# One core, hybrid decoder block: six levels of gated recurrence scores become two products of 192 queries, a step of the compression is moved, two slabs change places

## The reference, cut to what matters

```python
f = lb + (1.0 - lb) * jax.nn.sigmoid(f_logits)
logf, k = jnp.log(f), 1.0 - f
...
A = jnp.cumsum(lf, axis=2)
rel = jnp.where(tri[:, :, None], A[:, :, :, None, :] - A[:, :, None, :, :], -jnp.inf)
att = jnp.einsum('bhtd,bhsd,bhtsd->bhts', qq, kk, jnp.exp(rel))
o_intra = jnp.einsum('bhts,bhse->bhte', att, vv)
```

```python
ck = jnp.einsum('bcpgd,pde->bcge', kc[:, cidx] + pe_k[:, None, :], w_ck)
cv = jnp.einsum('bcpgd,pde->bcge', vc[:, cidx] + pe_v[:, None, :], w_cv)
```

## Time and profile before

| | us |
|---|---|
| median of 3 runs | 487.16 |
| lowest and highest | 487.15, 487.28 |
| the profiled execution, its own time | 487.02 |
| its span in the trace | 485.2 |
| PE busy | 476.9 (98%) |
| DVE busy | 341.4 (70%) |
| ACT busy | 264.3 (54%) |
| POOL busy | 158.1 (33%) |

### The profile page before, as it was taken

One profiled execution on the slowest core, in us unless ns is written; L12 is line 12 of the kernel. 1 busy time (PEld: TensorE's weight loads), 2 busy tenths in 40 slices (PEclk: granted clock), 3 DMA queues, 4 the chain that ended last, 5 costly groups with the idle time before them and its releaser, 6 DMA issues.

```text
span 485.2 us, 9672 instructions
## 1 busy us (share of the span) xinstructions
PE 476.9 (98%) x3974; PEld 465.2 (96%) x3974; DVE 341.4 (70%) x577; ACT 264.3 (54%) x397; POOL 158.1 (33%) x157
## 2 busy tenths in 40 slices
PE   9999999999999999999999999999999999999995
PEld 8999999999999999889999999999999999999995
DVE  4998967678976475797796747878584257655653
ACT  6887755286572737544565445576554245433531
POOL 1073810806200009990156424436745120000000
PEclk9999999999999999999999999999999999999999
DMA  9956552453453665455455344243525535677502
GB/s 294 337 173 192 178 173 63 132 169 109 154 174 95 198 145 174 122 172 179 147 161 187 92 125 134 88 140 122 169 94 174 173 117 188 218 228 249 174 1 86
DMA packets 77030, 76.43 MB, mean 158 GB/s; under 512 B 6783, under 2 KB 75775, under 8 KB 76987
## 3 DMA queue, kind: packets, MB, share of 16 engines
q1 hardware_dynamic: 76699, 75.64, 50.1%
q10 hardware_dynamic: 288, 0.18, 0.2%
HBM read 74.77 MB, written 1.05 MB: 156 GB/s over the span
## 4 chain that ended last, share of the span: by engine, by line
PE 94%; DVE 2%; ACT 2%; issue 1%; DVEq 0%; ACTq 0%
PE ps L986 75%; PE ps L1011 4%; PE ps L1154 3%; PE ps L1105 2%; PE ps L1094 1%; PE ps L1179 1%; PE ps L1173 1%; PE ps L1121 1%; DVE WL L621 1%; PE ps L1012 1%; PE ps L1108 1%; PE ps L1027 1%; PE ps L1122 1%; PE ps L1123 1%; PE ps L1054 1%
## 5 line engine op out<-in xcount | busy, mean ns | idle before, releaser
L986 PE MATMUL ps<-hH,WL 128*128 128x256 f32 x696 | 198.3, 289 | 0.9 <-DVE WL L621 0.9
L986 PE MATMUL ps<-hL,WH 128*128 128x256 f32 x696 | 197.0, 284 | 0.0
L986 PE MATMUL ps<-hH,WH 128*128 128x256 f32 x696 | 197.0, 284 | 0.0
L621 DVE TENSOR_TENSOR WL<-W,WH 128x2048 fp32r<-128x2048 f32 x66 | 152.9, 2316 | 19.6 <-PE ps L986 17.4
L427 ACT ACTIVATE WH<-W 128x2048 fp32r<-128x2048 f32 x66 | 124.6, 1888 | 44.8 <-PE ps L986 43.2
L986 PEld LDWEIGHTS ps<-hL,WH 128*128 128x128 f32 x696 | 132.8, 191 | 1.1 <-issue 1.0
L986 PEld LDWEIGHTS ps<-hH,WL 128*128 128x128 f32 x696 | 131.6, 191 | 2.3 <-DVE WL L621 1.1
L986 PEld LDWEIGHTS ps<-hH,WH 128*128 128x128 f32 x696 | 132.8, 191 | 0.0
L388 POOL TENSOR_SCALAR R<-R,st 128x256 f32<-128x256 f32 x32 | 29.2, 922 | 82.0 <-DVE st L797 82.0
L986 PE MATMUL ps<-bH,WL 128*128 128x256 f32 x192 | 54.9, 286 | 0.0
L986 PE MATMUL ps<-bH,WH 128*128 128x256 f32 x192 | 54.3, 283 | 0.0
(11 more groups left out here) (192 smaller groups left out, 776.9 us busy)
## 6 DMA issues: line engine op xcount, KB each, us to landing
W<-w_in SPq DMA_DIRECT2D x49, 1024.0 KB, 5.2
W<-w_branch SPq DMA_DIRECT2D x12, 1024.0 KB, 5.1
W<-w_out SPq DMA_DIRECT2D x4, 1024.0 KB, 5.8
R<-x SPq DMA_DIRECT2D x2, 512.0 KB, 4.6
W<-w_in SPq DMA_DIRECT2D x2, 512.0 KB, 6.7
R<-cmp_w SPq DMA_DIRECT2D x2, 512.0 KB, 8.3
OC<-pool_w SPq DMA_DIRECT2D x4, 256.0 KB, 5.9
...
```

The lines of the kernel that those rows point to most:

```text
L621: dve.tensor_tensor(WL[:, s % 2, :, 0:n], W[:, s % 3, :, 0:n], WH[:, s % 3, :, 0:n], ALU.subtract).then_inc(s_lo, 1)
L986: mm = pe.matmul(o, l, r, start=(at == 0 if mixed else k == 0 and j == 0), stop=(at == len(order) - 1 if mixed else k == KC - 1 and j == 2))
```

## The change

**Scores.** The levels 32, 16, 8, 4 become two steps of radix 4, with blocks of b = 16 and b = 4 tokens. In a group of four blocks, keys of block j reach queries of blocks j+1 to 3: six block pairs, so `REACH` holds 6b columns for 4b tokens, 192 for 128. `OWN` holds the keys. PE does two products of 192 queries, one of 64 (level 64, now in `HALF`) and one of 128 (blocks of 4, now into the next accumulator bank). Level 128 lies in `TOP`, in the tile `CVD`. POOL writes 4096 elements for a pair of heads in 12 instructions where it wrote 3584 in 12, and ACT's exponential takes 4096 where it took 3584.

**Compression.** ACT copies kc and vc out of the accumulator (`RAW`), and DVE builds the inputs from the copy in `late` of slabs 20 to 23 (`windows`), 4 additions in each.

**Order.** ks and kw become slabs 24 and 25, q3 slab 26. In slab 25 DVE does `lo(27)` ahead of `read(25)`. The copy of the compressed values (CV) moves from slab 28 to 27.

```diff
-LEVELS = (128, 64, 32, 16, 8, 4)
-NLV = len(LEVELS)
-SMALL_K, SMALL_Q = NLV, NLV + 1
+RADIX = (16, 4)
+STEPS = ((0, 3, 1), (3, 2, 2), (5, 1, 3))
...
-    out += [("q", n, "in", C_Q + n * SLAB) for n in (0, 1, 3)]
-    out += [("ks", 0, "in", C_KS), ("kw", 0, "in", C_KW)]
+    out += [("q", n, "in", C_Q + n * SLAB) for n in (0, 1)]
+    out += [("ks", 0, "in", C_KS), ("kw", 0, "in", C_KW), ("q", 3, "in", C_Q + 3 * SLAB)]
...
-CK, CV, CX, SC, TURN = 27, 28, 29, 31, 34
+CK, CV, CX, SC, TURN = 27, 27, 29, 31, 34
+WIN = 20
...
-                for i, b in enumerate(LEVELS):
...
+                b, n = 64, 2 * T // 128
...
+                for r, b in enumerate(RADIX):
+                    n = 2 * T // b
+                    av = a2.rearrange("p (n w) -> p n w", w=b)
+                    pool.tensor_tensor(OWN[p % 2][r].rearrange("p h (n w) -> p (h n) w", w=b),
+                                       k2.rearrange("p (n w) -> p n w", w=b),
+                                       av[:, :, b - 1:b].to_broadcast((P, n, b)), ALU.add)
+                    aw = a2.rearrange("p (n j w) -> p n j w", j=4, w=b)
+                    to = REACH[p % 2][r].rearrange("p h (n j w) -> p (h n) j w", j=6, w=b)
+                    for at, count, far in STEPS:
+                        pool.tensor_tensor(to[:, :, at:at + count], aw[:, :, far:4],
+                                           aw[:, :, 0:count, b - 1:b].to_broadcast((P, n // 4, count, b)), ALU.subtract)
...
-                        q = QK[p % 2]
-                        act.activation(q[:, 0, :, P:T], HA[:, 2 * p:2 * p + 2, P:T], ACT.Exp)
+                        act.activation(TOP[p % 2][:, :, P:T], HA[:, 2 * p:2 * p + 2, P:T], ACT.Exp)
                         for e in range(2):
...
+                        act.activation(DEC[p % 2], DEC[p % 2], ACT.Exp).then_inc(s_hexp, 1)
...
+                elif kind in ("kc", "vc"):
+                    act.activation(RAW[kind == "vc"], bank(s), ACT.Copy).then_inc(s_read_a, 1)
...
-                        for i, b in enumerate(LEVELS):
-                            ev = QK[h // 2 % 2][:, i, h % 2].rearrange("p (n w) -> p n w", w=2 * b)
+                        e, hp = h // 2 % 2, h % 2
+                        for b, to in ((128, TOP), (64, HALF)):
+                            ev = to[e][:, hp].rearrange("p (n w) -> p n w", w=2 * b)
                             qv = HQ[:, h].rearrange("p (n w) -> p n w", w=2 * b)
                             dve.tensor_tensor(ev[:, :, b:2 * b], ev[:, :, b:2 * b], qv[:, :, b:2 * b], ALU.mult)
-                        sq_ = QK[h // 2 % 2][:, SMALL_Q, h % 2]
+                        for r, b in enumerate(RADIX):
+                            qv = HQ[:, h].rearrange("p (n j w) -> p n j w", j=4, w=b)
+                            ev = REACH[e][r][:, hp].rearrange("p (n j w) -> p n j w", j=6, w=b)
+                            for at, count, far in STEPS:
+                                dve.tensor_tensor(ev[:, :, at:at + count], ev[:, :, at:at + count], qv[:, :, far:4],
+                                                  ALU.mult)
+                        sq_ = SMALL_Q[e][:, hp]
                         dve.tensor_tensor(sq_, sq_, HQ[:, h], ALU.mult).then_inc(s_hmul, 1)
...
                     link(dve.copy_predicated(PM[:, u % 2, 0:P], K[:, K_BLOCK:K_BLOCK + P].bitcast(mybir.dt.uint32),
-                                             ps[:, b0, K_BLOCK:K_BLOCK + P]))
-                    for lv in range(1, NLV):
-                        b = LEVELS[lv]
-                        r = slice(0, b if lv == 1 else P)
-                        to = PM[r, u % 2, 0:P].rearrange("p (n w) -> p n w", w=2 * b)[:, :, b:2 * b]
-                        c = slice(64 * (lv - 1), 64 * lv)
-                        last = dve.copy_predicated(to, K[r, c].bitcast(mybir.dt.uint32).rearrange(
-                            "p (n w) -> p n w", w=b), ps[r, b0, c].rearrange("p (n w) -> p n w", w=b))
-                        if lv < NLV - 1:
-                            link(last)
-                    last.then_inc(s_hmask, 1)
+                                             ps[:, b0 + 1, P:2 * P]))
+                    for r, b in enumerate(RADIX):
+                        c = slice(192 * r, 192 * r + 192)
+                        to = PM[:, u % 2, 0:P].rearrange("p (n j w) -> p n j w", j=4, w=b)
+                        on = K[:, c].bitcast(mybir.dt.uint32).rearrange("p (n j w) -> p n j w", j=6, w=b)
+                        src = ps[:, b0, c].rearrange("p (n j w) -> p n j w", j=6, w=b)
+                        for at, count, far in STEPS:
+                            link(dve.copy_predicated(to[:, :, far:4], on[:, :, at:at + count], src[:, :, at:at + count]))
+                    dve.tensor_copy(PM[0:64, u % 2, 64:P], ps[0:64, b0, 384:448]).then_inc(s_hmask, 1)
...
+            def windows(v, r):
+
+                dve.wait_ge(s_read_a, ACT_READS[WHERE[("vc" if v else "kc", 0)]])
+                pos = V[:, V_PEK + CB * v:V_PEK + CB * v + CB].rearrange("p (r j k) -> p r k j", r=2, k=2)
+                raw = RAW[v].rearrange("p (c t) -> p c t", c=2)
+                win = raw[:, :, CS * r:CS * r + CS * NCMP].rearrange("p q (c j k) -> p k j q c", j=CS // 2, k=2)
+                to = cpe[:, v, 8 * r:8 * r + 8].rearrange("p j (q e) c -> p e j q c", e=2)
+                for e in range(2):
+                    h = slice(64 * e, 64 * e + 64)
+                    for k in range(2):
+                        pv = pos[h, r, k].rearrange("p (j q c) -> p j q c", q=1, c=1)
+                        last = dve.tensor_tensor(to[64 * k:64 * k + 64, e], win[h, k],
+                                                 pv.to_broadcast((64, CS // 2, 2, NCMP)), ALU.add)
+                last.then_inc(s_win, 1)
+
             def late(s):
+                if WIN <= s < WIN + 4:
+                    windows((s - WIN) // 2, (s - WIN) % 2)
...
@@ -910,10 +933,12 @@
                 if mixing(s - 1):
                     lo(s + 1)
                 mix(s)
+                if s == WHERE[("kw", 0)]:
+                    lo(s + 2)
                 read(s)
                 if s == LAST:
                     merged_lo(3)
-                if s + 2 < NS and not mixing(s):
+                if s + 2 < NS and not mixing(s) and s != WHERE[("kw", 0)]:
                     lo(s + 2)
                 late(s)
...
-                q = QK[p % 2]
-                for lv in range(1, NLV):
-                    b = LEVELS[lv]
-                    t = q[:, lv, hp, P * i:P * i + P]
-                    up = t.rearrange("p (n w) -> p n w", w=2 * b)[:, :, b:2 * b]
-                    pe.matmul(ps[:, b0, 64 * (lv - 1):64 * lv], t, up, start=(lv == 1), stop=False)
-                mm = pe.matmul(ps[:, b0, K_BLOCK:K_BLOCK + P], q[:, SMALL_K, hp, P * i:P * i + P],
-                               q[:, SMALL_Q, hp, P * i:P * i + P], start=False, stop=True)
+                e, t = p % 2, slice(P * i, P * i + P)
+                for r in range(2):
+                    pe.matmul(ps[:, b0, 192 * r:192 * r + 192], OWN[e][r][:, hp, t],
+                              REACH[e][r][:, hp, 192 * i:192 * i + 192], start=(r == 0), stop=False)
+                pe.matmul(ps[:, b0, 384:448], HALF[e][:, hp, t], HALF[e][:, hp, P * i + 64:P * i + P],
+                          start=False, stop=True)
+                mm = pe.matmul(ps[:, b0 + 1, P:2 * P], SMALL_K[e][:, hp, t], SMALL_Q[e][:, hp, t],
+                               start=True, stop=(i == 0))
                 if i:
-                    mm = pe.matmul(ps[:, b0 + 1, 0:P], q[:, 0, hp, 0:P], q[:, 0, hp, P:T], start=True, stop=True)
+                    mm = pe.matmul(ps[:, b0 + 1, 0:P], TOP[e][:, hp, 0:P], TOP[e][:, hp, P:T], start=False, stop=True)
                 mm.then_inc(s_hp, 1)
...
-                pe.wait_ge(s_read_v, DVE_READS[WHERE[("vc", 0)]])
+                pe.wait_ge(s_win, 4)
```

More of the change, by code:

```diff
@@ L35 @@
 GATES = 3 * HEADS
-K_MASK, K_ID, K_ONE = 0, 448, 576
-K_BLOCK = K_MASK + 64 * (NLV - 1)
-K_CMASK, K_VALID, K_COUNT = 704, 734, 736
-K_ROWS, K_ALL = 800, 804
+K_MASK, K_BLOCK, K_ID, K_ONE = 0, 384, 512, 640
+K_CMASK, K_VALID, K_COUNT = 768, 798, 800
+K_ROWS, K_ALL = 864, 868
 K_CAUSAL = K_ALL
@@ L73 @@
 TOKEN_MAJOR = ("hv", "vs", "vw", "out")
-BY_ACT = ("f", "hq", "hv", "vs", "vw", "gate", "bv", "q", "ks", "kw", "silu", "merge", "out")
-BY_DVE = ("kc", "vc", "ks", "kw", "q", "silu", "branch", "out")
+BY_ACT = ("f", "hq", "hv", "vs", "vw", "gate", "kc", "vc", "bv", "q", "ks", "kw", "silu", "merge", "out")
+BY_DVE = ("ks", "kw", "q", "silu", "branch", "out")
 ACT_READS = [sum(x[0] in BY_ACT for x in SLABS[:i + 1]) for i in range(NS)]
@@ L147, in trunk @@
         HV = R[:, 3, :].rearrange("p (i n) -> p i n", i=TT)
-        QK = [R[:, 4 + 2 * b:6 + 2 * b, :].rearrange("p a (l h t) -> p (a l) h t", h=2, t=T) for b in range(2)]
+        DEC = [R[:, 4 + 2 * b:6 + 2 * b, :].rearrange("p a n -> p (a n)") for b in range(2)]
+        TOP = [CVD[:, 2 * b:2 * b + 2, :] for b in range(2)]
```

(32 more changed lines are left out.)

27 lines of the change are left out of this document (11 added, 16 removed).

## The result

The changed kernel took **489.23 us** (median of 6 runs, 487.75 to 489.75), the kernel before beside it 487.15 (6 runs, 487.00 to 487.28): ratio 1.0033, 95% interval 1.0021 to 1.0045. It is slower; 483.6 was forecast. The profiled execution took 489.32 us with a span of 487.5, 2.3 us more than before. The lowest of the six, 487.75, is still 0.6 above the kernel before.

What follows compares the result with a forecast made beforehand. PE, busy 98% of the span, was taken as the bound. Products -4.0, two waits -2.2, slab 25 +2.5 and slab 17 +0.1 sum to -3.6 us: 483.4 for the profiled execution, 483.6 median; range 482.4 to 485.0 (0.66).

Steps and rivals of the forecast that it cites:

- products, 16 units: PE's recurrence: each unit's half products take 1.09 us in place of 1.34, 0.25 less; 16 units give -4.0 us.
- stall at slab 17: DVE's added masks and multiplication before lo(17) use up its 2.2 us of slack, leaving a stall of 0.1 us.
- new stall at slabs 24 and 25: DVE's additions and masks make lo(25) late: PE stalls 2.5 us ahead of slab 25, a little already at slab 24.
- waits at slabs 28 and 29: PE's weight load waits for lo(28) and the copy of compressed values, 2.3 us; both go, taken as -2.2 us.
- The half product of 192 queries: PE's chain: priced at three quarters of the 256-query row, 0.162 us, with bounds of 0.112 and 0.216.
- a set of masks: DVE's masked copies for a unit: from 1.53 us to 2.06, +0.53 a unit, with bounds of +0.26 and +1.0.
- Columns alone: Rival on PE's products: price follows columns without a floor, +3.5 us in all, total 490.0 us; chance 0.01.
- ACT, POOL, SP: Other engines: longer exponential, two copies, POOL's about 1 us more and a delayed load are all covered, costing no time.
- +0.4 every second slab: DVE multiplying the queries in: four of six operations change width, 1.2 us for 0.8, so +0.4 us every second slab.
- That they now read a copy and not the accumulator I price at nothing.: DVE's compression additions in slabs 20 to 23: 4 a slab stay at 1.67 us though read from a copy.
- The order brings: Order of q3, ks, kw: both late waits go, -2.2 us; lo(26) hides behind slab 25's product of 5.75 us.
- my first rival: No new stall: cheaper additions from the copy and masks shorten DVE before lo(25) by 1.7 + 0.5 us; 481.3 us, chance 0.10.

Runs made afterwards that it cites:

- e1: Changed kernel with the compression additions for the keys both in slab 18, those for the values in slabs 20 and 21: 485.64 us, ratio 0.9956.
- e7: Changed kernel with ACT writing the copy of kc and vc in the order the additions read it: 486.16 us, ratio 0.9980.
- b1: Kernel before with the new order alone (ks, kw ahead of q3, values' copy in slab 27, lo(27) ahead of reading kw): 486.97 us, ratio 0.9988.
- b2: b1 with lo(26) ahead of reading ks: 484.86 us, ratio 0.9949.
- e2: Changed kernel with POOL's second pair of heads waiting until DVE has multiplied the queries into head 0: 486.27 us, ratio 0.9982.
- e5: Changed kernel with the edits of e1 and e2, and lo(26) ahead of reading ks: 482.20 us, ratio 0.9894.
- e8: e5 with POOL's first pair of heads waiting until DVE has prepared the third pair's gates: 481.40 us, ratio 0.9878.
- c1: e5 with one more set of four additions, a repetition, in slab 23: 486.21 us, ratio 0.9965, executions of two kinds.
- c2: e5 with repeated sets of additions, one more in slab 22 and three more in slab 23: 493.00 us, ratio 1.0115.
- e4: e1 with lo(26) ahead of reading ks: 483.43 us, ratio 0.9921.
- e3: Changed kernel with the edits of e1 and e2 together: 484.28 us, ratio 0.9927.
- e6: e5 with ACT writing the copy of kc and vc in the order the additions read it: 482.28 us, ratio 0.9896.

## Why the prediction was wrong, step by step

The differences between the traces at the slabs' starts, by the prediction's terms:

```
term                                    predicted   measured   by
products, 16 units                        -4.0        -3.8     chain; 0.24 a slab
stall at slab 17                          +0.1        +0.2     starts of slabs
new stall at slabs 24 and 25              +2.5        +3.9     starts; e1, e7
waits at slabs 28 and 29                  -2.2        -2.2     starts; b1, b2
late slab 9                                0          +1.5     e2, e5
late slab 5                                0          +0.3     e8
clock in slab 25                           0          +1.4     granted clock; c1, c2
silu's product, slab 30                    0          +0.4     only read, below
slab 1, and drift behind slab 32           0          +0.5     -
sum                                       -3.6        +2.2     span: +2.3
```

**Right.** The half product of 192 queries (0.163 us), the slab with a unit (7.30 us), a set of masks (2.07), the multiplication where nothing runs beside it (+0.4), the slack at slab 17, and the place of the new stall. Columns alone didn't set the price, as the forecast held. That a unit saves 0.24 us hides two misses that cancel, though: the two half products of 64 and the two of 128 were priced at 0.22 us a pair, and the chain has 0.17 and 0.28.

**The first step that failed: "ACT, POOL, SP", priced at nothing.** I checked that POOL's *fourth* pair ends 4.9 us before ACT wants it. I never asked what the *second* pair runs beside. DVE's multiplication for head 0 took 4.4 us there already before the change (53.11 to 57.50), nearly three times its price in a quiet slab, with `lo(9)` done at 60.3 and 2.7 us of slack. In the changed kernel the multiplication takes 7.6 us, and the slack is overrun by 1.5. e2 moves only POOL's pair and gets it back; e5 against e4 repeats it (1.2 us). The "+0.4 every second slab" was right where POOL was idle, and wrong by 2.8 us for the first head.

**The second step that failed: "That they now read a copy and not the accumulator I price at nothing."** It costs 0.17 us for each addition, 0.66 for a set, two sets ahead of `lo(25)`. e7 takes this back and the stalls shrink from 3.9 us to 2.6, about the 2.5 that I forecast with the lower price. I had argued from the time for an element; but the tile row that I compared with the earlier trace rows reads runs of neighbouring elements, and the copy is read at every sixteenth. e2 and e7 each mend one of the two steps alone, and each brings the changed kernel's median about 1 us below the kernel before (0.9982 and 0.9980). It took both, and the clock, to make it slower.

**The clock.** That a stall can cost more than its length was in no term. In the profile it is 1.4 us; among the changed kernel's executions the one without it took 487.75, the others 488.92 or more, with a mean granted clock of 0.998 against 0.994 or 0.995. In all groups of runs the same mark tells the slower executions of a kernel from the others: a mean granted clock of 0.996 or less, against 0.997 or more. By the stall at slab 25 they go like this. Without one (e1, e3 to e6, b1, b2, e8, which have at most a stall of 1.9 us at slab 26) none of 45 executions has the mark. With 2.3 us (c1) 7 of 12 have it, with 2.4 (e7) 1 of 11, with 3.0 (e2 and the changed kernel) 5 of 12 and 5 of 6, with 7.7 (c2) all four. c1 and c2 change nothing but the stall, and so show that a stall can bring the dip. The Trainium skill's page "TensorE: Matmul & The Clock Gate", section "HAM oscillation — how this bites in real kernels", says that gaps in PE's work bring the clock down for the work behind them; the profiles of the changed kernel and c2 agree, those of e2, e7 and c1, with stalls of 2.3 to 3.0 us and no dip, don't show it. What decides it for one execution and not the next is open, and the stall's length alone does not: the kernel before, with two waits of 1.1 us, has the mark in 10 of its 61 executions in all (6 of 23, 1 of 9, 3 of 23, none of 6), 1.1 to 1.7 us above the median. In which slab those lose it no profile shows.

**"The order brings" -2.2 us.** This term was right in the changed kernel by luck, for I had the reason wrong. I let `lo(26)` hide behind the product of slab 25, and counted DVE's four readings of ks (2.8 us) but not ACT's four copies ahead of them (2.4). b1 shows that it doesn't hide: the order brings +1.9 at slab 26 with it, and is worth 0.3 us by itself. The stall that I had forecast at slab 25 covered this. Had that stall not come, as in my first rival, slab 26 would have started 1.9 us late instead, as e1 shows.

**The 0.4 us at slab 30** are only read, not tested: silu's product of two tiles (L868) takes 1.4 us in the profiles of the changed kernel and e1, beside one of POOL's, and 0.69 in e4, where POOL's comes later. b1 and e3 have the 1.4 too.

The best version found, e8, keeps the change and adds four small edits of order: 481.4 us, 1.2% below the kernel before.
